# The seven block products of the feed-forward groups in a new order, with another opening and another turn into the down projection

## The reference

```python
x = x + 0.5 * swiglu(rmsnorm(x, ffn1_norm), ffn1_w_gate, ffn1_w_up, ffn1_w_down)
u = rmsnorm(x, mix_norm)
proj = u @ w_in            # -> RG-LRU heads and SSD heads, each with conv and scan
x = x + jnp.concatenate([lru_out, ssd_out], axis=-1) @ w_out
x = x + 0.5 * swiglu(rmsnorm(x, ffn2_norm), ffn2_w_gate, ffn2_w_up, ffn2_w_down)
# swiglu: (silu(x @ w_gate) * (x @ w_up)) @ w_down ; D_MODEL = 1024, D_FF = 2816
```

## Time and profile before

| | us |
|---|---|
| median of 3 runs (range) | 2204.09 (2202.66 to 2207.38) |
| the profiled execution | 2212.14 |
| its span | 2210.2 |
| PE busy in the span | 2140.0 (97%) |
| DVE busy | 1462.6 (66%) |
| POOL busy | 1225.7 (55%) |
| ACT busy | 593.7 (27%) |

### The profile page before, as it was taken

The page is one execution under the profiler, slowest core; times in us unless marked ns, Lnnn a source line. Parts: engine busy times, 40 slices in busy tenths (PEclk is TensorE's granted clock), DMA queues, the critical chain, the costliest instruction groups (busy, mean ns, idle before and its releaser), DMA issues.

```text
span 2210.2 us, 36672 instructions
## 1 busy us (share of the span) xinstructions
PE 2140.0 (97%) x15504; PEld 2105.7 (95%) x15504; DVE 1462.6 (66%) x1259; ACT 593.7 (27%) x856; POOL 1225.7 (55%) x825
## 2 busy tenths in 40 slices
PE   6999999988999999899999999999999999989998
PEld 5989999988999999889999999999999999989998
DVE  7797778763222567877888596787888777642215
ACT  5211101111000224577877540122100101110003
POOL 7778888872442322325352663335988888824340
PEclk8999999999999999999999999999999999989999
DMA  4122222226321322311110422132212222363222
GB/s 146 58 77 79 76 77 97 73 101 220 96 73 58 111 93 90 120 65 51 40 60 31 173 87 89 48 116 77 69 67 97 77 77 78 108 221 90 82 58 77
DMA packets 64755, 197.84 MB, mean 90 GB/s; under 512 B 9416, under 2 KB 18120, under 8 KB 64592
## 3 DMA queue, kind: packets, MB, share of 16 engines
q1 hardware_dynamic: 63440, 194.97, 26.0%
q10 hardware_dynamic: 1152, 0.52, 0.1%
HBM read 149.37 MB, written 46.26 MB: 89 GB/s over the span
## 4 chain that ended last, share of the span: by engine, by line
PE 78%; DVE 8%; DVEq 4%; ACT 3%; DMA 2%; issue 2%; POOL 1%; POOLq 1%; ACTq 0%; SPq 0%
PE banks L770 41%; PE banks L850 30%; PE banks L1117 2%; PE banks L815 2%; DMA stage<-hidden 2%; POOLq L663 1%; DVEq L1577 1%; DMA hidden<-up 1%; DVEq L1594 1%; DVE rstd L1538 1%; DVEq L1555 1%; DVE mix L1559 0%; POOL w L664 0%; DVEq L1558 0%; DVE h_lo L1640 0%
## 5 line engine op out<-in xcount | busy, mean ns | idle before, releaser
L623 POOL TENSOR_SCALAR w_hi<-w_raw 128x1024 fp32r<-128x1024 f32 (+1 forms) x93 | 106.6, 1146 | 597.2 <-PE banks L770 531.4
L625 POOL TENSOR_TENSOR w_lo<-w_raw,w_hi 128x1024 fp32r<-128x1024 f32 (+1 forms) x100 | 270.3, 2703 | 162.2 <-DVE xbc L1886 123.4
L770 PE MATMUL banks<-h_hi,w_lo 128*128 128x344 f32 x948 | 306.2, 323 | 14.4 <-DVE x L1672 14.4
L770 PE MATMUL banks<-h_lo,w_hi 128*128 128x344 f32 x948 | 304.9, 322 | 0.0
L770 PE MATMUL banks<-h_hi,w_hi 128*128 128x344 f32 x948 | 304.8, 322 | 0.0
L770 PE MATMUL banks<-u_hi,w_lo 128*128 128x344 f32 x864 | 286.4, 331 | 6.4 <-issue 6.1
L770 PE MATMUL banks<-u_hi,w_hi 128*128 128x344 f32 x864 | 276.4, 320 | 0.0
L770 PE MATMUL banks<-u_lo,w_hi 128*128 128x344 f32 x864 | 276.0, 319 | 0.0
L1672 DVE SCALAR_TENSOR_TENSOR x<-banks,x 128x1032 f32<-128x1032 f32 x42 | 51.7, 1232 | 301.3 <-PE banks L770 301.3
L1197 ACT ACTIVATE parts<-banks 128x516 f32<-128x516 f32 x80 | 47.6, 597 | 659.1 <-PE banks L850 659.1
L770 PEld LDWEIGHTS banks<-h_hi,w_lo 128*128 128x128 f32 x948 | 180.0, 190 | 15.0 <-DVE x L1672 15.0
(11 more groups left out here) (353 smaller groups left out, 5953.4 us busy)
## 6 DMA issues: line engine op xcount, KB each, us to landing
w_raw<-in_gate_up SPq DMA_DIRECT2D x46, 512.0 KB, 4.3
hidden<-up SPq DMA_DIRECT2D x44, 516.0 KB, 6.2
stage<-hidden SPq DMA_DIRECT2D x44, 516.0 KB, 3.6
raw<-in_gate_up SPq DMA_DIRECT2D x40, 512.0 KB, 4.6
w_raw<-in_w_in SPq DMA_DIRECT2D x36, 512.0 KB, 4.2
w_raw<-in_down SPq DMA_DIRECT2D x32, 512.0 KB, 3.9
x<-in_xt SPq DMA_DIRECT2D x16, 516.0 KB, 6.6
x_kept<-x SPq DMA_DIRECT2D x16, 516.0 KB, 5.1
```

The source lines that it names most:

```text
L623: pool.tensor_scalar(w_hi[s][:, 0:n], w_raw[s][:, 0:n], 1.0, 0.0, ALU.mult, ALU.add)
L625: pool.tensor_tensor(w_lo[s][:, 0:n], w_raw[s][:, 0:n], w_hi[s][:, 0:n].bitcast(F32), ALU.subtract).then_inc(split, 1)
L770: end = pe.matmul(out[:, c, 0:CH], w[s][:, k * P:(k + 1) * P], x[kx][:, c * CH:(c + 1) * CH], start=(first and n == 0), stop=(last and n = ...
```

## The change

1. **Order of the products**: p1, p2, p6, p5, p7, p3, p4 in every group, the first of each block too. Both products that come first use x itself.
2. **Joins**: ACT copies only p1 (`part`). DVE reads every other product out of PSUM itself (`join`): seven adds from PSUM a group (p7 is read twice), where there were five from PSUM and two between SBUF tiles. Half of the scaling goes ahead of p4.
3. **Plain units** in three chunks of 344 columns over three banks, not four of 258. ACT copies three of the four outputs in one instruction each; DVE takes the last out of PSUM by its scaling, after the reciprocal, and counts it as the fourth of `taken`. In f1 the third product of group 0 waits for that, in f2 the second. `norm_sum` goes before k = 6, not k = 4.
4. **Opening of f1**: TensorE does all products with high x first and those with low x after. ACT makes all eight high parts, then four squares; the other squares come later. The seven additions of squares go from POOL to DVE, after `mixes`. ACT takes the plain outputs between the mixes, in f2 too.
5. **Turn**: four stage tiles, not two (the other two are the raw weight tiles 0 and 1); hidden tiles 2 and 3 are loaded early, and 4 to 7 may each follow four behind. `hidden_low` of tiles 0 to 7 goes between the joins of the last group, one or two behind each, and two after p4. Tiles of x are loaded again earlier and in another order; in f1 x tile 3 still goes between the last store and the wait for it, x 4 and 7 behind the wait; in f2 all before the last store.
6. DVE's preparation of `lam` is spread over groups 1 to 4, `prepare_history` goes from group 2 to 5 and `prepare_steps` from 3 to 6. In the middle `decode_scale(5)` and z's first scaling go ahead of `decode(4)`.

The core of the diff:

```diff
+STEADY = ("p1", "p2", "p6", "p5", "p7", "p3", "p4")
+READ = {STEADY: ("p2", "p6", "p5", "p7", "p3", "p4")}
+def order(q):
+    return STEADY
+def stage_of(j):
+    return (j % 4, j // 4) if j < 8 else (j % 2, 2 + (j - 8) // 2)
...
             def load_hidden(f, j):
-                if j >= 2:
-                    sp.wait_ge(*f.hidden.past(j - 1))
+                if j >= 4:
+                    sp.wait_ge(*f.hidden.past(j - 3 if j < 8 else j - 1))
...
                 store_hidden(f, NG // 2 - 1)
+                x_again(f, src, 2)
+                if tag == "2":
+                    x_again(f, src, 7)
+                sp.wait_ge(*f.op_ready.past(7 * (NG - 1)))
+                for j in range(2, 4):
+                    load_hidden(f, j)
...
+                sp.wait_ge(*f.done.past(NOPS))
+                x_again(f, src, 0)
+                x_again(f, src, 1)
+                sp.wait_ge(*f.hidden.past(8))
+                x_again(f, src, 5)
+                x_again(f, src, 6)
+                if tag == "2":
+                    sp.wait_ge(*f.ev.past(6 * NG))
+                    x_again(f, src, 3)
+                    x_again(f, src, 4)
+                store_hidden(f, NG // 2)
                 if tag == "1":
...
+                    x_again(f, src, 3)
+                sp.wait_ge(*f.h_stored.past(32 * (NG // 2 + 1)))
+                if tag == "1":
+                    x_again(f, src, 4)
+                    x_again(f, src, 7)
...
+                    elif o == (1 if f.tag == "1" else 0):
+                        pe.wait_ge(*f.rooted.past(1))
+                    if o == (2 if f.tag == "1" else 1):
+                        pe.wait_ge(*f.taken.past(4))
+                    if o == 2:
+                        pe.wait_ge(*f.mix_lo.past(4))
...
             for k in range(AHEAD, KT):
-                as_it_comes(g, gate, k)
-                as_it_comes(u, up, k)
+                highs(g, gate, k)
+                highs(u, up, k)
+            for k in range(KT):
+                low(g, gate, k)
+            for k in range(KT):
+                low(u, up, k)
...
             def plain_pair(f):
-                dve.wait_ge(*f.taken.past(8))
                 for tile in f.g:
                     last = dve.tensor_tensor(tile[:], tile[:], rstd[:], ALU.mult)
                 last.then_inc(f.scaled.sem, 1)
-                for tile in f.u:
-                    dve.tensor_tensor(tile[:], tile[:], rstd[:], ALU.mult)
+                dve.tensor_tensor(f.u[0][:], f.u[0][:], rstd[:], ALU.mult)
+                dve.wait_ge(used, U(("u" + f.tag, 1)) + 1)
+                dve.tensor_tensor(cut(f.u[1][:]), f.u_at, cut(rstd[:]), ALU.mult).then_inc(f.taken.sem, 1)
                 hidden_pair(f, 0)
...
+                dve.wait_ge(*f.copied.past(q + 1))
+                join("p2", part, c11)
+                join("p6", part, c21)
+                join("p5", c21, part)
+                join("p7", part, c22, (c21, c21))
+                join("p3", part, c12)
+                dve.drain()
+                if not last:
+                    dve.tensor_tensor(dst[0][:], dst[0][:], rstd[:], ALU.mult)
+                return lambda: join("p4", c21, c21)
...
+            for k in range(4):
+                mixes(f1, k, V_FFN1)
+            for k in range(1, KT):
+                dve.wait_ge(squared["ffn1"], k + 1)
+                dve.drain()
+                dve.tensor_tensor(f1.tot[:], f1.tot[:], f1.c[k % 3][:], ALU.add).then_inc(added["ffn1"], 1)
             for k in range(4):
                 mix_low(f1, k)
```

More of the change, by code:

```diff
@@ L219, in build, with ffn_tiles @@
         f1 = Names()
-        def ffn_tiles(f, tag, x, tt, bb, gate, up, raw, op, sums, parts, stage, late):
+        def ffn_tiles(f, tag, x, tt, bb, gate, up, raw, op, sums, stage, late):
             f.tag, f.x = tag, at(f"x{tag}", x, [KT, T])
@@ L232, in ffn_tiles @@
             f.s = [at(f"w_sum{tag}_{n}", sums, [512], skip=512 * n) for n in range(3)]
-            four = at(f"parts{tag}", parts, [4, HT])
-            f.p = [four[:, n, :] for n in range(4)]
-            f.stage = [at(f"stage{tag}_{n}", tile, [T]) for n, tile in enumerate(stage)]
+            f.p = at(f"part{tag}", sums, [HT], skip=3 * 512)
+            f.stage = [at(f"stage{tag}_{n}", tile, [T]) for n, tile in enumerate(stage + raw)]
             h = [(bb + 4 * k, bb + 4 * k + 1) for k in range(4)] + [(tt + 4 * k, tt + 4 * k + 2) for k in range(4)]
@@ L464, in down @@
                     load(("d" + tag, 0, m))
-                for j in range(2, 8):
+                for j in range(4, 8):
                     load_hidden(f, j)
@@ L887, in tensor, with highs @@
             for _ in range(12):
-                pe.matmul(pair[:, 0, 0:P], ones[:], ones[:], start=True, stop=True)
+                pe.matmul(banks[:, 0, 0:P], ones[:], ones[:], start=True, stop=True)
             g, u = plan.u(("g1", 0)), plan.u(("u1", 0))
             gate, up = f1.g_at, f1.u_at
-            def as_it_comes(unit, out, k):
+            def highs(unit, out, k):
                 if k == 0:
@@ L1226, in group @@
                     end.then_inc(f.silu.sem, 1)
-                part(f, q, 1)
-                if last:
-                    for j in range(2, 8):
-                        hidden_high(f, j)
             def groups_and_down(f, extra):
@@ L1600, in corners, with join @@
             def corners(f, q, between=None):
+                last = q == NG - 1
                 dst = f.u if q % 2 else f.g
+                c11, c12, c21 = dst[0][:, 0:HT], dst[0][:, HT:T], dst[1][:, 0:HT]
+                c22, part = dst[1][:, HT:T], f.p[:]
+                def join(name, a, to, second=None):
+                    o = number(q, name)
+                    dve.wait_ge(*f.done.past(o + 1))
+                    dve.drain()
+                    end = dve.tensor_tensor(halved(to), twos[o % 4], halved(a), ALU.add)
+                    if second:
+                        end = dve.tensor_tensor(halved(second[1]), twos[o % 4], halved(second[0]), ALU.add)
+                    end.then_inc(f.ev.sem, 1)
+                    if between and name in between:
+                        between[name]()
```

326 lines of the change are left out of this document (139 added, 187 removed).

## The result

The changed kernel takes 2167.07 us (median of 4 runs, 2165.77 to 2169.70) where the kernel before took 2204.03 (4 runs, 2202.66 to 2207.38): ratio 0.9832, interval 0.9815 to 0.9849, 37.0 us less. Measured beside each other on another occasion, the changed kernel took 2168.65 us and the kernel before 2211.16: ratio 0.9808, interval 0.9794 to 0.9821, 42.5 us less. The forecast was 43.8 us less, 2160.3. The profiled execution of after took 2166.39 us, 45.8 less than that of before.

A forecast was written before the change was run, and what follows sets the result against it. TensorE was taken as the bound, busy 2140 of 2210.2 us, with some 70 us idle. Gains 6.4 + 8.5 + 16.0 + 15.9 - 4.0 + 1.0 = 43.8 us, off 2204.1, gave 2160.3 us; range 2147 to 2178.

The forecast's parts named there:

- its excess of 8 us over the median is taken as common to both kernels: Whole kernel: the profiled 2212.1 us lay 8 us above the median in either kernel, so 43.8 came off 2204.1.
- nothing changes: Rival for the whole kernel: new waits at group 0 (11.5 and 7.7 us idle) and their clock eat the gain; chance 0.03.
- DVE as the bound of the groups: Rival in the 40 steady groups: joins stretched to 1.78 us make DVE the limit, 2232 us, slower; chance 0.04.
- Opening of f1, 6.4 foretold: Start of f1 to group 0's third product: starts at 75.9, not 84.7, gain 8.8 less 2.4 for low clock.
- Group 2, 8.5 foretold: Group 2 of f1: 5.7 us of waits plus 2.8 at half clock go, as lam comes in pieces; at least 4.
- 2.5 us are free: Steady groups, p2's read after a hidden pair: DVE takes 11.9 us behind p4's end, TensorE needs the bank at 14.4.
- about 14.4: Steady groups: DVE's load per group in us after the change, from 15.6 before, in a group of 20.2.
- Turns, 16.0 and 15.9 foretold: f1's and f2's turns into the down projection: m = 2 starts 13.4 and 13.2 us earlier, clock adds 2.6 and 2.7.
- Opening of f2, -4.0 foretold: Start of f2: second product 1.6 us later, 2.4 lost to clock behind 7.7 us idle; bounds +1 and -7.
- The middle, 1 foretold: Wait of 6.07 us before the middle's slots: gain of 1 us, bounds -1 and 6.
- One 1.2 us scaling moves ahead: Middle, before the slots: one 1.2 us scaling goes ahead of a long decode, the reason given for 1 us gain.

## Why the prediction was right, and where it wasn't

**The total.** 43.8 us foretold; 45.6 between the profiled spans, 42.5 and 37.0 between the medians on two occasions. The one wrong step at this level is "its excess of 8 us over the median is taken as common to both kernels": the kernel before lies at 2204 or at 2210 from one occasion to the next (medians 2204.0, 2210.7, 2211.2, 2204.4, 2210.1), the changed one at 2167 to 2169. What was subtracted from 2204.1 belonged to an execution of 2212, so the forecast of 2160.3 came out 6.8 us below the 2167.1 measured. The rival "nothing changes" and DVE as the bound of the groups are out.

**Opening of f1, 6.4 foretold, 6.0 measured.** The third product starts at 76.70 and not 75.9. DVE's links came as put together, some errors cancelling: additions end at 48.9 (46.7 foretold), low mixes at 59.85 (59.7), the scaling from PSUM at 76.6. u1 ended at 60.4 and not 58.6, after the 1.69 us of wait for POOL at 20.90 that the sum left out; DVE's longer chain hid it.

**Group 2, 8.5 foretold, 5.9 measured.** The step that failed is the room: "2.5 us are free" and DVE at "about 14.4" us a group. The ten groups above have 163.22 us of DVE, 16.3 a group, and the same ten of before 15.65: the load rose. The joins kept their price, as reasoned; two-input work in SBUF did not. The groups of instructions of DVE in after, 145.3 to 470.3 us (xcount, busy, mean ns, idle before), then the scaling in before that takes the place of the second row, 145.3 to 488.6 us:

```profile
L1622 DVE TENSOR_TENSOR up<-banks,part 128x516 f32<-128x516 f32 x34 | 23.6, 696 | 32.3 <-PE banks L887 30.5 <-issue 0.2
L1639 DVE TENSOR_TENSOR up<-up,rstd 128x1032 f32<-128x1032 f32 x8 | 18.8, 2353 | 0.7
```

```profile
L1633 DVE TENSOR_TENSOR up<-up,rstd 128x1032 f32<-128x1032 f32 x8 | 9.9, 1233 | 0.7
```

A join from PSUM takes 0.70 us beside POOL, now as before. The four kinds of scaling between SBUF tiles took 1.23 to 2.34 us in before, 1.71 on average; in after they take 2.14 to 2.35, 2.25 on average, and 1.23 in f1's turn, where POOL is nearly quiet. With two of them a group that is 1.1 us, and the four weight sums of a group cost 0.65 more (1.32 and not 1.16 each); the adds gave 1.1 back. So a preparation of 1 to 2 us in an even group, where DVE also makes a hidden pair, was already too much: 1.26 and 1.30 us of wait in groups 2 and 6, gone when the preparations stand in odd groups.

**Turns, 16.0 and 15.9 foretold, 15.0 and 15.4 measured.** m = 2 needed the residual 12.5 and 12.7 us earlier (13.4 and 13.2), and the clock behind gave 2.5 and 2.7 (2.6 and 2.7). The reasons given hold as far as they were tried: without the extra stage tiles half of it is gone. Where DVE's four splits stand doesn't matter with four stage tiles.

**Opening of f2, -4.0 foretold, -3.0 measured.** Wait 7.83 for 7.7; the clock cost 1.8 to 1.9 and not 2.4.

**The middle, 1 foretold, 6.4 measured.** The mis-sized term. "One 1.2 us scaling moves ahead" is what the edit does, 1.1 us in the kernel before, but undoing it in the changed kernel cost nothing. By the traces the wait went because two clashes of DVE with POOL's splits were missed, one 22 us ahead of the slots and one just before the z tiles; the prediction had neither. The 6.4 us lie above its upper bound of 6.

The terms missed in both directions, -2.6 in group 2 and +5.4 in the middle; that the total of 43.8 is nearer than its parts is luck.

## What to carry to other kernels

A wait that an edit takes from one engine is worth what the next link on the slowest engine's chain allows: in f1's opening the wait before the third product only went to the fifth and sixth or to the next group, while in f2's an earlier sum and the scaling that TensorE waits for put first took it away. Price what DVE has free in a group from the busy time of the changed mix of work, SBUF pairs at their stretched price, and put odd jobs where the group has no other. And before a profiled execution is set against a median, look whether the kernel's runs form one cluster, on more than one occasion.

## What the runs showed of the hardware

A DVE addition of two SBUF tiles (128x1024) took 1.23 us when it began 0.35 us ahead of POOL's split and 2.11 when it began with it, the next operation 1.89 against 3.25 (rows above): who began first decided some 2 us, in every one of the profiles the same way. POOL's split took 1.05 where it began with the addition and 1.79 where the addition was ahead. The Trainium skill ("SBUF — State Buffer", "Who interferes with whom") says that a DVE instruction with two SBUF inputs contends with a GpSimd instruction that reads SBUF, by an exclusive lock, and one with at most one SBUF input does not. The rows on either side agree, and so do the joins from PSUM, which stay at 0.70.

The granted clock can fall behind waits of only 0.3 us where small matmuls come thinly: in the middle of the changed kernel TensorE does 54 matmuls in the 8 us from 793 to 801, and waits 0.35 us at 792.86 and 0.30 us at 803.63. Behind these two waits, the same instructions of the same kernel, after and then its repetition:

```profile
803.60:811.60 8.00, 7.97 (x102) 7.95 (x103) 5.58 (x7) 3.32 (x4) 1.15 (x1) 1.00 0.58 164
```

```profile
804.70:812.70 8.00, 8.00 (x93) 7.98 (x94) 5.55 (x7) 3.42 (x4) 0.00 (x0) 0.79 0.57 157
```

At 0.79 it is nine matmuls fewer in 8 us, and the way from m = 2 of f1 to the middle's slots took 399.2 us and not 397.6. In five of the ten profiles of the changed kernel and its variants the clock fell there, in five it did not; 1.6 of the 4 us over which its runs scatter would be this.
